# A 31-tap convolution as even and odd outputs that share three half-length filters, with one input buffer

## The chip, the cores and the metric

The kernel runs on one core of a Trainium2 chip. The metric is the device time of one launch in microseconds, as the median of several runs. The core's engines work side by side, each through its own list of instructions, and wait for each other through semaphores: TensorE (PE, matrix products), VectorE (DVE, elementwise work on 128 partitions), ScalarE (ACT, activation functions and copies), GpSimd (POOL, here small square roots and the stores), and SyncE (SP), which issues the loads.

## The reference

One inference step of a two-layer encoder trunk: 2048 prompt frames and 64 sample frames, 1024 channels. Layer 0 is the one that the change touches:

```python
def conv_mixer(h, hist, w_in, conv_w, conv_b, ln_g, ln_b, w_out):
    p = h @ w_in
    a, g_glu, z = jnp.split(p, 3, axis=-1)
    c = a * jax.nn.sigmoid(g_glu)
    c_pad = jnp.concatenate([hist.astype(c.dtype), c], axis=1)
    y = causal_dwconv(c_pad, conv_w, conv_b)          # 31 taps, each channel by itself
    y = jax.nn.silu(layernorm(y, ln_g, ln_b)) * jax.nn.silu(z)
    return y @ w_out, c_pad[:, -CONV_STATE:]
```

Layer 1 is a gated unit with three large products (`u`, `v`, `z`) and a 128x128 mixing of frames. Both layers have a norm before and behind, and a residual sum. All is float32; each large product is made as three products of a high and a low half.

## The kernel before

The frames are cut into two halves: half 0 has 1024 frames (8 tiles of 128), half 1 has 1024 + 64 (9 tiles). Frames lie along the free dimension in the stages A and U, channels on the partitions.

- **Stage A** (to about 600 us) computes the input product of layer 0 in 48 units, n = 0 to 47, 24 for each half. A unit is 128 output channels; three in a row make one block of 128 channels: the sigmoid part (n mod 3 = 0), the linear part (1), whose product with the sigmoid VectorE makes (`cs`, L1074), and `z` (2). A unit has two chunks of 512 frames in half 0 and three of 364, 364 and 360 in half 1. Its weights are loaded (`raw`), rounded by ScalarE to a high half (`Wh`, `a_high`) and subtracted by VectorE for the low half (`Wl`, `a_low(n + 2)`, in unit n). The block is stored to `c_scratch`.
- **The convolution** works on 16 blocks, 8 channel groups for each half. A block is loaded into `cp` (two buffers), 1024 columns wide in half 0 and 1118 in half 1 (prompt, history and sample frames in one). VectorE adds tap by tap into `acc` (two buffers): the first tap is a TENSOR_SCALAR with the bias (L1049), the 30 others are a SCALAR_TENSOR_TENSOR, shifted source times weight plus `acc` (L1053). Each waits for the one before. The block is then stored to `y_scratch` by GpSimd.
- **The plan** (`tap_plan`) spreads the 16x31 taps over VectorE's instruction list: in stage A 3 taps in the units 4 and 5, 7 in the units 6 to 43, 4 in 44 and 45; in stage V 2 or 3 for each tile; in stage U 11 for each `j`. VectorE runs them in that place and in no other.
- **Stage O** follows for half 0: norm, gate and output product of layer 0, tile by tile. Its first pieces are drawn into the last units of stage A: the statistic `o_stats(0, 0)` stands on VectorE right behind the taps of unit 43, and TensorE's second group of transposes of tile 0 stands behind the first chunk of unit 44.
- **Stage V** for half 0 (about 705 to 880 us) computes `v` in four quarters of 8 tiles. VectorE has the low half of the next quarter's weights (`Vl`), the taps and a statistic (`vbs`, L1206) for each tile.
- **Stage U** for half 0 (to about 1280 us) has 16 steps `j`: the products for `u` and `z`, the norm of `v` on VectorE (`vt`, L1224 and L1228), the mixing on TensorE (L1573), the gating (`m`, L1257 and L1272), and taps at three places.
- Then the stages O, V and U of half 1 and the last output product, in which there is no convolution.

SyncE issues the loads in a list of its own. `c_load(b + 2)` stands in the unit where block b ends, behind the weight load of that unit, and waits for block b's last tap. GpSimd's stores of `y` stand likewise in the unit where a block ends.

Of the kernel before, what the change touches and what calls it, by code (L numbers as in the profile page):

```python
# [5 lines left out]
P = 128  # L6
# [20 lines left out]
NCH = (2, 3)  # L27
UNITS_A = 3 * JA
CONV_W = (1024, 1024 + HIST + N_SAMPLE)
NBLK = 2 * JA  # L30
VW = 512
NQ = EB // VW

P_CONVB, P_LNG, P_LNB, P_BG, P_BB = 0, 8, 16, 24, 40
# [4 lines left out]
    return N_SAMPLE if t == NTILES - 1 else P  # L39


def tap_plan():
# [5 lines left out]
    taps, ends, k = {}, {}, 0  # L48
    for key, n in room:
        hi = min(k + n, NBLK * TAPS)  # L50
        taps[key] = (k, hi)
        for b in range(NBLK):
            if k <= TAPS * b + TAPS - 1 < hi:
                ends.setdefault(key, []).append(b)
        k = hi
    assert k == NBLK * TAPS
    return taps, ends


def build(nc, x, wa_in, wa_out, wb_v, wb_uz, wb_out, hist, conv_w, chan_par, pre_g, post_g, b_gb, ws_t, s_bias,  # L60
# [14 lines left out]
    with ctx:  # L75
# [16 lines left out]
        def sem(name):  # L92
            return ctx.enter_context(nc.semaphore(name))
# [5 lines left out]
        par = g("par", [P, NPAR])  # L99
# [30 lines left out]
        r = Region(r1_at, r2_at)  # L130
# [6 lines left out]
        for h in range(2):  # L137
            r = Region(r2_at, c_at)
# [50 lines left out]
        for h in range(2):  # L189
            o = OutBuffers()  # L190
            r = Region(m_at, w_at) if h == 0 else Region(c_at, m_at)
            o.yb = [r(f"yb{h}{i}", [P, KD, P]) for i in range(3)]

            at = r.at
            o.zb, o.sl = [r(f"zb{h}0", [P, KD, P])], [Region(at, top)(f"sl{h}0", [P, KD, P], f32r)]
            o.sh = [r(f"sh{h}0", [P, KD, P], f32r)]
            at = z1_at if h == 0 else m_at
            o.zb.append(Region(at, top)(f"zb{h}1", [P, KD, P]))
            o.sl.append(Region(at, top)(f"sl{h}1", [P, KD, P], f32r))
            r = Region(e_at, top) if h == 0 else Region(m_at + KD * P * 4, w_at)  # L200
            o.xn = [r(f"xo{h}{i}", [P, D]) for i in range(2)]
            r = Region(w_at, e_at)
# [59 lines left out]
        a_cld = [sem(f"a_cld{i}") for i in range(2)]  # L262
        a_yst = [sem(f"a_yst{i}") for i in range(2)]
# [31 lines left out]
        taps_at, conv_ends = tap_plan()  # L295


        def x_slot(t):
# [117 lines left out]
        def _(sp):  # L416
# [10 lines left out]
            def c_load(b):  # L427
                h, j = b // JA, b % JA
                sp.wait_ge(a_cst, c_stored(b))
                if b >= 2:  # L430
                    sp.wait_ge(a_conv, b - 1)
                if h == 0:
                    sp.dma_start(cp[b % 2][:, HIST:HIST + 1024], c_d[j, :, HIST:HIST + 1024]).then_inc(a_cld[b % 2], 16)
                else:
                    sp.wait_ge(ld_hist, 16)
                    sp.dma_start(cp[b % 2][:, :], c_d[j, :, 1024:PADDED]).then_inc(a_cld[b % 2], 16)

            def c_loads(key):
                for b in conv_ends.get(key, []):
                    if b + 2 < NBLK:  # L440
                        c_load(b + 2)

            def wo_load(h, k):
                if k == 0 and h == 0:
# [5 lines left out]
            def o_load_y(t):  # L450
                h = half_of(t)
                if t == TILES[h][0]:
                    for s in range(2):
                        sp.wait_ge(a_yst[s], y_stored(JA * (h + 1) - 2 + s))
# [165 lines left out]
            for n in range(2 * UNITS_A):  # L620
                if n + 3 < 2 * UNITS_A:
                    a_load(n + 3)
                if n == 2:
                    c_load(0)
                for i in (2 * n, 2 * n + 1):
                    if 11 + i < NTILES:
                        x_load(11 + i)
                if n == 5:
                    c_load(1)
# [32 lines left out]
        def _(pool):  # L662
# [26 lines left out]
            def y_stores(key):  # L689
                for b in conv_ends.get(key, []):  # L690
                    h, j = b // JA, b % JA
                    pool.wait_ge(a_conv, b + 1)
                    full, tail = tiled(y_d, h, j)
                    a = acc[b % 2]
                    nc.gpsimd.dma_start(full, a[:, 0:1024].rearrange("p (t n) -> p t n", n=P)).then_inc(a_yst[b % 2], 16)
                    if h == 1:
                        nc.gpsimd.dma_start(tail, a[:, 1024 + HIST:CONV_W[1]]).then_inc(a_yst[b % 2], 16)

            def ln_rsqrt(t):
                pool.wait_ge(o_agg, t + 1)  # L700
# [314 lines left out]
        def _(dve):  # L1015
# [24 lines left out]
            def taps(k0, k1):  # L1040
                for i in range(k0, k1):
                    b, k = i // TAPS, i % TAPS
                    h, j = b // JA, b % JA
                    a, c, w = acc[b % 2][:, 0:CONV_W[h]], cp[b % 2], CONV_W[h]
                    if k == 0:
                        dve.wait_ge(a_cld[b % 2], 16 * (b // 2 + 1))
                        if b >= 2:
                            dve.wait_ge(a_yst[b % 2], y_stored(b - 2))
                        ins = nc.vector.tensor_scalar(a, c[:, 0:w], cw[:, j, 0:1], par[:, P_CONVB + j:P_CONVB + j + 1],  # L1049
                                                      ALU.mult, ALU.add)  # L1050
                    else:
                        dve.wait_ge(a_tap, (TAPS - 1) * b + k)
                        ins = nc.vector.scalar_tensor_tensor(out=a, in0=c[:, k:k + w], scalar=cw[:, j, k:k + 1], in1=a,  # L1053
                                                             op0=ALU.mult, op1=ALU.add)
                    ins.then_inc(a_conv if k == TAPS - 1 else a_tap, 1)

            def fill(key):
                taps(*taps_at.get(key, (0, 0)))

            def a_chunk(n, c):  # L1060
                h, j, m = unit_a(n)
                c0, w = CHUNKS[h][c]
                p = a_pos[n, c]
                k0, k1 = taps_at.get(("A", n), (0, 0))
                taps(k0 + (k1 - k0) * c // NCH[h], k0 + (k1 - k0) * (c + 1) // NCH[h])
                if c == (1 if n < 3 else 0):
                    if 3 <= n + 2 < 2 * UNITS_A:
                        a_low(n + 2)
                    if 26 <= n < 26 + KD:
                        wo_low(0, n - 26)  # L1070
                if m == 1:
                    dve.wait_ge(a_sig, a_count(n - 1, c))
                    dve.wait_ge(a_mm, p + 1)
                    nc.vector.tensor_tensor(cs[:, c0:c0 + w], PS[:, p % A_BANKS, 0:w], cs[:, c0:c0 + w], ALU.mult)\  # L1074
                        .then_inc(a_prod, 1)
                if 0 <= p - 2 < 9:
                    n1_low(6 + p)
                    if 7 + p < NTILES:
                        n1_scale(7 + p)
# [237 lines left out]
            for t in range(8):  # L1317
# [2 lines left out]
                    a_low(t // 2)  # L1320
                if t + 2 < 9:
                    n1_scale(t + 2)
            for i in range(2):
                nc.vector.memset(cp[i][:, 0:HIST], 0.0).then_inc(c_pad, 1)
            dve.wait_ge(ld_par, 16)
            dve.wait_ge(ld_cw, 16)
            dve.wait_ge(c_pad, 2)
# [369 lines left out]
```

## Time and profile before

| | |
|---|---|
| median of 3 runs | 2417.61 us (2415.47 to 2418.39) |
| the profiled execution, its own time | 2414.95 us |
| its span in the profile | 2413.1 us |
| TensorE busy | 2351.5 us, 97% |
| VectorE busy | 1449.3 us, 60% |
| ScalarE busy | 674.6 us, 28% |
| the taps L1053 | 480 operations, 639.4 us |
| granted TensorE clock, mean | 0.99 |

The profile shows for each engine what it did and when, and for each idle stretch what ended it. An arrow as in `PS L1573 <- DVE vt L1228` names who was waited for: here TensorE's work of line 1573 waited for VectorE's result `vt` of line 1228. TensorE is the busiest engine, so a stretch in which it waits is time lost; waits of the others cost nothing by themselves.

### The profile page before, as it was taken

How to read it: one execution, taken by the hardware profiler on the slowest of the kernel's cores; microseconds unless marked ns; L12 is line 12 of the kernel's file. 1: busy time of each engine (PE TensorE's matmuls, PEld its weight loads, DVE VectorE, ACT ScalarE, POOL GpSimd, SP SyncE). 2: the span in 40 equal slices, each digit the busy share in tenths (PEclk: the TensorE clock that was granted, in tenths of full speed). 3: DMA queues.
4: the chain of work that ended last, by engine and by line, in shares of the span. 5: the costliest groups of instructions: out<-in, count | busy, mean ns of one | idle time of the engine just before them, and what ended most of it. 6: DMA issues, size and time to landing. Idle time of an engine off the chain costs nothing.

```text
span 2413.1 us, 27653 instructions
## 1 busy us (share of the span) xinstructions
PE 2351.5 (97%) x11824; PEld 2053.7 (85%) x11824; DVE 1449.3 (60%) x1395; ACT 674.6 (28%) x955; POOL 233.4 (10%) x419
## 2 busy tenths in 40 slices
PE   7899999999999998999989999999999998999998
PEld 6788899999887887888778877889999998888885
DVE  5599999995769879999946742224334444222221
ACT  5322223222542112222324531112222333111110
POOL 1100000001211110000001210011000000000000
PEclk9999999999999999999989999999999999999999
DMA  4323244232552213333334442113222344322220
GB/s 167 122 93 100 98 136 143 94 125 76 185 192 104 95 68 106 112 101 113 126 120 140 137 147 95 65 53 100 85 86 89 116 135 166 110 97 91 92 92 22
DMA packets 113818, 265.05 MB, mean 110 GB/s; under 512 B 15776, under 2 KB 51872, under 8 KB 111648
## 3 DMA queue, kind: packets, MB, share of 16 engines
q1 hardware_dynamic: 90208, 184.64, 23.3%
q0 software_dynamic: 23488, 78.64, 9.5%
q8 instruction: 93, 1.52, 0.3%
q14 instruction: 29, 0.24, 0.0%
HBM read 184.86 MB, written 78.75 MB: 109 GB/s over the span
## 4 chain that ended last, share of the span: by engine, by line
PE 92%; DVE 4%; DMA 2%; ACT 1%; issue 1%; POOL 0%; SPq 0%; DVEq 0%; ACTq 0%
PE PS L1366 29%; PE PS L1367 29%; PE PS L1368 29%; PE PS L1573 3%; DVE acc L1053 2%; PE PS L1412 1%; PE PS L1434 1%; PE PS L1377 1%; DMA raw<-wa_in_in 0%; PE PS L1421 0%; DMA zb<-silu_z_scratch 0%; DMA xt<-x_in 0%; DVE m L1272 0%; DMA rawb<-wb_out_in 0%; DVE Ul L1017 0%
## 5 line engine op out<-in xcount | busy, mean ns | idle before, releaser
L1053 DVE SCALAR_TENSOR_TENSOR acc<-cp,cw,acc 128x1024 f32<-128x1024 f32 (+1 forms) x480 | 639.4, 1332 | 12.6
L1366 PE MATMUL PS<-HBh,Uh 128*128 128x512 f32 (+2 forms) x1280 | 457.6, 357 | 1.6 <-ACT vb L931 1.6
L1367 PE MATMUL PS<-HBl,Uh 128*128 128x512 f32 (+2 forms) x1280 | 453.4, 354 | 0.0
L1368 PE MATMUL PS<-HBh,Ul 128*128 128x512 f32 (+2 forms) x1280 | 453.4, 354 | 0.0
L1366 PE MATMUL PS<-HAh,Wh 128*128 128x512 f32 (+2 forms) x960 | 341.7, 356 | 0.5 <-DVE HAl L1017 0.5
L1367 PE MATMUL PS<-HAl,Wh 128*128 128x512 f32 (+2 forms) x960 | 340.0, 354 | 0.0
L1368 PE MATMUL PS<-HAh,Wl 128*128 128x512 f32 (+2 forms) x960 | 339.8, 354 | 0.0
L1366 PEld LDWEIGHTS PS<-HBh,Uh 128*128 128x128 f32 x1280 | 241.9, 189 | 23.4 <-issue 2.6
L1368 PEld LDWEIGHTS PS<-HBh,Ul 128*128 128x128 f32 x1280 | 241.6, 189 | 20.7
L1367 PEld LDWEIGHTS PS<-HBl,Uh 128*128 128x128 f32 x1280 | 241.8, 189 | 20.0 <-issue 0.2
L1366 PE MATMUL PS<-Wbh,s7h 128*128 128x512 f32 (+1 forms) x544 | 212.6, 391 | 7.4 <-DVE s7l L1017 7.4
L1366 PE MATMUL PS<-Vh,HBh 128*128 128x512 f32 (+1 forms) x544 | 212.5, 391 | 1.8 <-DVE Vl L1017 1.7
L1367 PE MATMUL PS<-Wbl,s7h 128*128 128x512 f32 (+1 forms) x544 | 212.5, 391 | 0.0
L1368 PE MATMUL PS<-Wbh,s7l 128*128 128x512 f32 (+1 forms) x544 | 212.2, 390 | 0.0
L1367 PE MATMUL PS<-Vl,HBh 128*128 128x512 f32 (+1 forms) x544 | 211.8, 389 | 0.0
L1368 PE MATMUL PS<-Vh,HBl 128*128 128x512 f32 (+1 forms) x544 | 211.7, 389 | 0.0
L1366 PEld LDWEIGHTS PS<-HAh,Wh 128*128 128x128 f32 x960 | 181.4, 189 | 15.8 <-issue 0.7
L1368 PEld LDWEIGHTS PS<-HAh,Wl 128*128 128x128 f32 x960 | 181.1, 189 | 15.3
L1367 PEld LDWEIGHTS PS<-HAl,Wh 128*128 128x128 f32 x960 | 181.3, 189 | 14.8
L1353 DVE TENSOR_TENSOR t<-PS,gpb 128x1024 f32<-128x1024 f32 (+1 forms) x17 | 20.8, 1224 | 238.5 <-ACT t7b L797 238.5
L1206 DVE BATCH_NORM_STATS2 vbs<-vb 128x6 f32<-128x512 f32 (+1 forms) x68 | 47.1, 692 | 153.9 <-ACT vb L931 153.7
L947 ACT ACTIVATE sz<-PS 128x512 f32<-128x512 f32 (+2 forms) x80 | 41.8, 523 | 338.6 <-PE PS L1368 338.6
(116 smaller groups left out, 3036.6 us busy)
## 6 DMA issues: line engine op xcount, KB each, us to landing
rawu<-wb_uz_in SPq DMA_DIRECT2D x64, 512.0 KB, 3.5
raw<-wa_in_in SPq DMA_DIRECT2D x48, 512.0 KB, 3.5
rawv<-wb_v_in SPq DMA_DIRECT2D x64, 256.0 KB, 4.8
v_scratch<-vb POOLq DMA_DIRECT2D x64, 256.0 KB, 2.6
vt<-v_scratch SPq DMA_DIRECT2D x32, 512.0 KB, 4.0
s_scratch<-m POOLq DMA_DIRECT2D x32, 512.0 KB, 3.9
st<-s_scratch SPq DMA_DIRECT2D x16, 1024.0 KB, 4.9
xt<-x_in SPq DMA_DIRECT2D x16, 512.0 KB, 4.4
```

Of the source, the lines that this page charges most:

```text
L947: nc.scalar.activation(to[:, c0:c0 + w], PS[:, u_bank(h, p), 0:w], (ACT.Gelu, ACT.Silu)[m])\
L1053: ins = nc.vector.scalar_tensor_tensor(out=a, in0=c[:, k:k + w], scalar=cw[:, j, k:k + 1], in1=a, op0=ALU.mult, op1=ALU.add)
L1206: nc.vector.bn_stats(vbs[0:m, i, q, :], vb[u % 5][0:m, :]).then_inc(v_bn, 1)
L1353: nc.vector.tensor_tensor(t7[0:n, :], banks(2 * b_pair(t))[0:n, :], gpb[0:n, :], ALU.mult).then_inc(b_pm, 1)
L1366: nc.tensor.matmul(out, wh, xh, start=start, stop=False)
L1367: nc.tensor.matmul(out, wh, xl, start=False, stop=False)
L1368: return nc.tensor.matmul(out, wl, xh, start=False, stop=stop)
L1377: last = nc.tensor.transpose(banks(b)[:, k * P:k * P + n], xn[t % 2][0:n, k * P:(k + 1) * P], ident[0:n, 0:n])
L1412: last = nc.tensor.transpose(PS[0:n, 6, k * P:(k + 1) * P], y[:, 4 * half + k, 0:n], ident)
L1434: last = nc.tensor.transpose(banks(4)[:, k * P:k * P + n], ob[half_of(t)].xn[t % 2][0:n, k * P:(k + 1) * P], ident[0:n, 0:n])
L1573: last = nc.tensor.matmul(PS[:, mix_at[h] + i // 4, i % 4 * P:i % 4 * P + n], vt[0:n, i, :], wst[0:n, j // 2, 0:n], start=True, stop=True)
```

## The change

The 31-tap filter is split by the parity of its taps: 16 even ones and 15 odd ones. For each block, with m half the width (512 or 559):

- `pair` is the sum of neighbouring inputs on m + 15 columns (one TENSOR_TENSOR, both sources take every second element).
- The even filter adds 16 taps on m + 1 columns of even inputs into the first half of `acc`; the odd filter adds 15 taps on m columns of odd inputs into the second half. Both read `cp` at every second element, and their first operation is a TENSOR_SCALAR.
- Even outputs: first half + bias + second half, written to every second element of `yc`.
- Odd outputs: `over` = first half moved by one - bias + second half, and then 16 steps with the sums of neighbouring weights (`cg`, made once) on `pair`, the first subtracting `over`; the last writes every second element of `yc`.

That is 50 steps a block on half the columns, where there were 31 on all. All but `pair` wait for the one before them. `cp`, `acc` and the output `yc` are one buffer each: the load of block b + 1 waits until block b has read `cp` for the last time (32 steps done), and block b writes `yc` only when the store of b - 1 has landed. The plan gives 6 steps to the units 4 and 5, 13 to the units 6 to 43, none to 44 and 45; 3 for each tile of stage V's first quarter and 5 in the others; 5, 6 and 6 for each `j` of stage U, until the 800 are done.

```diff
-    room = [(("A", n), 3 if n < 6 else 4 if n >= 44 else 7) for n in range(4, 2 * UNITS_A - 2)]
-    room += [(("V", q, i), 2 if q == 0 or i % 2 == 0 else 3) for q in range(NQ) for i in range(8)]
-    room += [(("U", j, part), n) for j in range(KB) for part, n in enumerate((3, 4, 4))]
+    room = [(("A", n), 6 if n < 6 else 13) for n in range(4, 2 * UNITS_A - 4)]
+    room += [(("V", q, i), 3 if q == 0 else 5) for q in range(NQ) for i in range(8)]
+    room += [(("U", j, part), n) for j in range(KB) for part, n in enumerate((5, 6, 6))]
...
-        cp = [r(f"cp{i}", [P, CONV_W[1] + HIST]) for i in range(2)]
-        acc = [r(f"acc{i}", [P, CONV_W[1]]) for i in range(2)]
+        cp = r("cp", [P, CONV_W[1] + HIST + 2])
+        acc = r("acc", [P, CONV_W[1] + 2])
+        pair = r("pair", [P, CONV_W[1] // 2 + EVEN])
+        over = r("over", [P, CONV_W[1] // 2])
+        yc = r("yc", [P, CONV_W[1]])
...
             def c_load(b):
                 h, j = b // JA, b % JA
                 sp.wait_ge(a_cst, c_stored(b))
-                if b >= 2:
-                    sp.wait_ge(a_conv, b - 1)
+                if b >= 1:
+                    sp.wait_ge(a_tap, (STEPS - 1) * (b - 1) + AT_Y0)
...
+                def taken(at, n):
+                    return cp[:, at:at + 2 * n - 1:2]
+
+                def filtered(out, first, src, w, start):
+                    if start:
+                        return nc.vector.tensor_scalar(out, src, w, None, ALU.mult)
+                    return nc.vector.scalar_tensor_tensor(out=out, in0=src, scalar=w, in1=first, op0=ALU.mult, op1=ALU.add)
+
+                if k == 0:
+                    if b >= 1:
+                        dve.wait_ge(a_conv, b)
+                    dve.wait_ge(a_cld, 16 * (b + 1))
+                    ins = nc.vector.tensor_tensor(pair[:, 0:m + ODD], taken(1, m + ODD), taken(2, m + ODD), ALU.add)
+                else:
+                    dve.wait_ge(a_tap, (STEPS - 1) * b + k)
+                if AT_EVEN <= k < AT_ODD:
+                    i = k - AT_EVEN
+                    ins = filtered(q0, q0, taken(2 * i, m + 1), cw[:, j, 2 * i:2 * i + 1], i == 0)
+                if AT_ODD <= k < AT_Y0:
+                    i = k - AT_ODD
+                    ins = filtered(q1, q1, taken(2 * i + 1, m), cw[:, j, 2 * i + 1:2 * i + 2], i == 0)
+                if k == AT_Y0:
+                    if b >= 1:
+                        dve.wait_ge(a_yst, c_stored(b - 1))
+                    ins = nc.vector.scalar_tensor_tensor(out=yc[:, 0:2 * m:2], in0=acc[:, 0:m], scalar=bias, in1=q1,
+                                                         op0=ALU.add, op1=ALU.add)
+                if k == AT_OVER:
+                    ins = nc.vector.scalar_tensor_tensor(out=over[:, 0:m], in0=acc[:, 1:m + 1], scalar=bias, in1=q1,
+                                                         op0=ALU.subtract, op1=ALU.add)
+                if k >= AT_BOTH:
+                    i = k - AT_BOTH
+                    w = cg[:, j, i:i + 1] if i < ODD else cw[:, j, TAPS - 1:TAPS]
+                    out = over[:, 0:m] if i < ODD else yc[:, 1:2 * m:2]
+                    ins = nc.vector.scalar_tensor_tensor(out=out, in0=pair[:, i:i + m], scalar=w, in1=over[:, 0:m],
+                                                         op0=ALU.mult, op1=ALU.subtract if i == 0 else ALU.add)
+                ins.then_inc(a_conv if k == STEPS - 1 else a_tap, 1)
```

## Rows read from the trace of the kernel before

**Rows 1.** The page: busy time of each engine, its share, instructions.

```profile
PE 2351.5 (97%) x11824; PEld 2053.7 (85%) x11824; DVE 1449.3 (60%) x1395; ACT 674.6 (28%) x955; POOL 233.4 (10%) x419
```

**Rows 2.** TensorE's waits over the span: us in total, times, longest.

```profile
PE PS L1573 <- DVE vt L1228: 8.5, 2, 6.2
...
PE PS L1421 <- DVE rm L1103: 4.9, 1, 4.9
PE PS L1412 <- DVE bst L1095: 4.1, 2, 3.5
PE PS L1366 <- DVE Vl L1017: 1.7, 1, 1.7
```

**Rows 3.** Busy time by stretch, stage A: PE, PEld, DVE, ACT, POOL, clock, DMA.

```profile
121.50:551.30 429.80, 429.80 (x2288) 397.55 (x2287) 401.69 (x344) 109.03 (x132) 31.39 (x45) 1.00 0.33 111
```

**Rows 4.** Groups by form: VectorE's taps and a short operation; busy us, mean ns.

```profile
L1053 DVE SCALAR_TENSOR_TENSOR acc<-cp,cw,acc 128x1118 f32<-128x1118 f32 x240 | 331.4, 1381 | 5.8
L1053 DVE SCALAR_TENSOR_TENSOR acc<-cp,cw,acc 128x1024 f32<-128x1024 f32 x240 | 307.9, 1283 | 6.7
...
L1247 DVE SCALAR_TENSOR_TENSOR addj<-rsb,par,sbb 128x128 f32<-128x128 f32 x32 | 11.0, 344 | 0.0
...
L1049 DVE TENSOR_SCALAR acc<-cp,cw,par 128x1024 f32<-128x1024 f32 x8 | 6.5, 808 | 0.0
```

**Rows 5.** VectorE in order of time, stage A: start, us, operation, [idle before].

```profile
46.75 1.22 DVE L1017 TENSOR_TENSOR HAl<-PS,HAh 128x1024 fp32r<-128x1024 f32 x1 [1.98 <-ACT HAh L810]
...
120.40 1.23 DVE L1017 TENSOR_TENSOR Wl<-raw,Wh 128x1024 fp32r<-128x1024 f32 x1 [3.44 <-ACT Wh L814]
...
219.47 9.20 DVE L1053 SCALAR_TENSOR_TENSOR acc<-cp,cw,acc 128x1024 f32<-128x1024 f32 x7
228.58 1.22 DVE L1017 TENSOR_TENSOR Wl<-raw,Wh 128x1024 fp32r<-128x1024 f32 x1
...
550.60 0.69 DVE L1095 BATCH_NORM_STATS2 bst<-PS 128x6 f32<-128x512 f32 x1
```

**Rows 6.** VectorE's waits from 121.5 to 320 us.

```profile
DVE Wl L1017 <- ACT Wh L814: 8.9, 11, 3.4
```

**Rows 7.** VectorE's waits from 320 to 551.3 us.

```profile
DVE Wl L1017 <- ACT Wh L814: 11.6, 10, 1.9
DVE Wol L1017 <- ACT Woh L842: 3.7, 2, 2.7
```

**Rows 8.** TensorE in order of time, at two places.

```profile
552.93 0.60 PE L1412 MATMUL PS<-con,yb 128*128 128x128 f32 x4
...
923.01 3.78 PE L1573 MATMUL PS<-wst,vt 128*128 128x128 f32 x16 [6.23 <-DVE vt L1228]
```

**Rows 9.** Busy time by stretch behind the longest stop; the clock is third from last.

```profile
919.00:923.00 4.00, 0.00 (x0) 0.00 (x0) 3.93 (x5) 0.00 (x0) 0.00 (x0) 0.50 0.58 219
923.00:929.20 6.20, 6.19 (x23) 5.65 (x24) 6.13 (x7) 0.00 (x0) 1.51 (x2) 0.51 0.15 42
```

**Rows 10.** VectorE in order of time, stage V: first quarter, then a later one.

```profile
728.40 0.67 DVE L1017 TENSOR_TENSOR Vl<-rawv,Vh 128x512 fp32r<-128x512 f32 x1
...
732.31 0.68 DVE L1017 TENSOR_TENSOR Vl<-rawv,Vh 128x512 fp32r<-128x512 f32 x1
...
809.47 0.69 DVE L1206 BATCH_NORM_STATS2 vbs<-vb 128x6 f32<-128x512 f32 x1 [0.87 <-ACT vb L931]
...
814.91 0.69 DVE L1206 BATCH_NORM_STATS2 vbs<-vb 128x6 f32<-128x512 f32 x1
```

**Rows 11.** VectorE in order of time, stage U.

```profile
906.00 1.28 DVE L1257 SCALAR_TENSOR_TENSOR m<-PS,par,addj 128x1024 f32<-128x1024 f32 x1 [5.54 <-PE PS L1573]
...
921.73 1.23 DVE L1228 TENSOR_TENSOR vt<-vt,vrs 128x1024 f32<-128x1024 f32 x1
...
956.28 1.27 DVE L1257 SCALAR_TENSOR_TENSOR m<-PS,par,addj 128x1024 f32<-128x1024 f32 x1
...
980.10 1.28 DVE L1257 SCALAR_TENSOR_TENSOR m<-PS,par,addj 128x1024 f32<-128x1024 f32 x1
...
1222.07 1.23 DVE L1017 TENSOR_TENSOR Ul<-rawu,Uh 128x1024 fp32r<-128x1024 f32 x1 [4.33 <-ACT Uh L904]
```

**Rows 12.** DMA issues: a block's load and store; KB each, us from issue to landing.

```profile
y_scratch<-acc POOLq DMA_DIRECT2D x16, 512.0 KB, 4.5
...
cp<-c_scratch SPq DMA_DIRECT2D x8, 512.0 KB, 4.4
```

More of the change, by code:

```diff
@@ L12 @@
 TAPS = 31
+EVEN, ODD = 16, 15
 HIST = TAPS - 1
@@ L30 @@
 NBLK = 2 * JA
+AT_EVEN, AT_ODD = 1, 1 + EVEN
+AT_Y0 = AT_ODD + ODD
+AT_OVER, AT_BOTH = AT_Y0 + 1, AT_Y0 + 2
+STEPS = AT_BOTH + EVEN
 VW = 512
@@ L39, in rows, with conv_plan @@
     return N_SAMPLE if t == NTILES - 1 else P
-def tap_plan():
-    room = [(("A", n), 3 if n < 6 else 4 if n >= 44 else 7) for n in range(4, 2 * UNITS_A - 2)]
-    room += [(("V", q, i), 2 if q == 0 or i % 2 == 0 else 3) for q in range(NQ) for i in range(8)]
-    room += [(("U", j, part), n) for j in range(KB) for part, n in enumerate((3, 4, 4))]
-    taps, ends, k = {}, {}, 0
+def conv_plan():
+    room = [(("A", n), 6 if n < 6 else 13) for n in range(4, 2 * UNITS_A - 4)]
+    room += [(("V", q, i), 3 if q == 0 else 5) for q in range(NQ) for i in range(8)]
+    room += [(("U", j, part), n) for j in range(KB) for part, n in enumerate((5, 6, 6))]
+    steps, read, ends, k = {}, {}, {}, 0
     for key, n in room:
-        hi = min(k + n, NBLK * TAPS)
-        taps[key] = (k, hi)
+        hi = min(k + n, NBLK * STEPS)
+        steps[key] = (k, hi)
         for b in range(NBLK):
-            if k <= TAPS * b + TAPS - 1 < hi:
+            if k <= STEPS * b + AT_Y0 - 1 < hi:
+                read.setdefault(key, []).append(b)
+            if k <= STEPS * b + STEPS - 1 < hi:
                 ends.setdefault(key, []).append(b)
         k = hi
-    assert k == NBLK * TAPS
-    return taps, ends
+    assert k == NBLK * STEPS
+    return steps, read, ends
 def build(nc, x, wa_in, wa_out, wb_v, wb_uz, wb_out, hist, conv_w, chan_par, pre_g, post_g, b_gb, ws_t, s_bias,
@@ L161, in build @@
         r = Region(c_at, m_at)
[L162 to L163 removed]
+        cp = r("cp", [P, CONV_W[1] + HIST + 2])
[3 more added lines that the diff above has]
+        yc = r("yc", [P, CONV_W[1]])
         cw = r("cw", [P, JA, TAPS])
+        cg = r("cg", [P, JA, ODD])
         r = Region(m_at, top)
@@ L261, in build @@
         a_cst, a_zst, a_tap, a_conv = (sem(f"a_{n}") for n in ("cst", "zst", "tap", "conv"))
-        a_cld = [sem(f"a_cld{i}") for i in range(2)]
-        a_yst = [sem(f"a_yst{i}") for i in range(2)]
+        a_cld, a_yst = sem("a_cld"), sem("a_yst")
         out_conv = sem("out_conv")
@@ L293, in build @@
         b_st = [sem(f"b_st{i}") for i in range(3)]
-        taps_at, conv_ends = tap_plan()
+        steps_at, conv_read, conv_ends = conv_plan()
         def x_slot(t):
@@ L429, in c_load @@
                 sp.wait_ge(a_cst, c_stored(b))
-                if b >= 2:
-                    sp.wait_ge(a_conv, b - 1)
+                if b >= 1:
+                    sp.wait_ge(a_tap, (STEPS - 1) * (b - 1) + AT_Y0)
                 if h == 0:
-                    sp.dma_start(cp[b % 2][:, HIST:HIST + 1024], c_d[j, :, HIST:HIST + 1024]).then_inc(a_cld[b % 2], 16)
+                    sp.dma_start(cp[:, HIST:HIST + 1024], c_d[j, :, HIST:HIST + 1024]).then_inc(a_cld, 16)
                 else:
                     sp.wait_ge(ld_hist, 16)
-                    sp.dma_start(cp[b % 2][:, :], c_d[j, :, 1024:PADDED]).then_inc(a_cld[b % 2], 16)
+                    sp.dma_start(cp[:, 0:CONV_W[1] + HIST], c_d[j, :, 1024:PADDED]).then_inc(a_cld, 16)
             def c_loads(key):
-                for b in conv_ends.get(key, []):
-                    if b + 2 < NBLK:
-                        c_load(b + 2)
+                for b in conv_read.get(key, []):
+                    if b + 1 < NBLK:
+                        c_load(b + 1)
             def wo_load(h, k):
@@ L452, in o_load_y @@
                 if t == TILES[h][0]:
-                    for s in range(2):
-                        sp.wait_ge(a_yst[s], y_stored(JA * (h + 1) - 2 + s))
+                    sp.wait_ge(a_yst, c_stored(JA * (h + 1) - 1))
                     if h == 0:
@@ L693, in y_stores @@
                     full, tail = tiled(y_d, h, j)
-                    a = acc[b % 2]
-                    nc.gpsimd.dma_start(full, a[:, 0:1024].rearrange("p (t n) -> p t n", n=P)).then_inc(a_yst[b % 2], 16)
+                    nc.gpsimd.dma_start(full, yc[:, 0:1024].rearrange("p (t n) -> p t n", n=P)).then_inc(a_yst, 16)
                     if h == 1:
-                        nc.gpsimd.dma_start(tail, a[:, 1024 + HIST:CONV_W[1]]).then_inc(a_yst[b % 2], 16)
+                        nc.gpsimd.dma_start(tail, yc[:, 1024 + HIST:CONV_W[1]]).then_inc(a_yst, 16)
             def ln_rsqrt(t):
@@ L1038, in wo_low, with conv_step @@
                 split_low(Wol[:, k, :], rawo[:, k, :], Woh[:, k, :], wo_lo)
-            def taps(k0, k1):
-                for i in range(k0, k1):
[L1042 to L1055, printed above, removed]
+            def conv_step(b, k):
+                h, j = b // JA, b % JA
+                m = CONV_W[h] // 2
+                q0, q1, bias = acc[:, 0:m + 1], acc[:, m + 1:2 * m + 1], par[:, P_CONVB + j:P_CONVB + j + 1]
+                def taken(at, n):
[32 more added lines that the diff above has]
+                ins.then_inc(a_conv if k == STEPS - 1 else a_tap, 1)
@@ L1057, in fill, with conv_steps @@
+            def conv_steps(k0, k1):
+                for i in range(k0, k1):
+                    conv_step(i // STEPS, i % STEPS)
             def fill(key):
-                taps(*taps_at.get(key, (0, 0)))
+                conv_steps(*steps_at.get(key, (0, 0)))
             def a_chunk(n, c):
@@ L1063, in a_chunk @@
                 p = a_pos[n, c]
-                k0, k1 = taps_at.get(("A", n), (0, 0))
-                taps(k0 + (k1 - k0) * c // NCH[h], k0 + (k1 - k0) * (c + 1) // NCH[h])
+                k0, k1 = steps_at.get(("A", n), (0, 0))
+                conv_steps(k0 + (k1 - k0) * c // NCH[h], k0 + (k1 - k0) * (c + 1) // NCH[h])
                 if c == (1 if n < 3 else 0):
@@ L1322, in _ @@
                     n1_scale(t + 2)
-            for i in range(2):
-                nc.vector.memset(cp[i][:, 0:HIST], 0.0).then_inc(c_pad, 1)
+            for i, n in ((0, HIST), (CONV_W[0] + HIST, 2), (CONV_W[1] + HIST, 2)):
+                nc.vector.memset(cp[:, i:i + n], 0.0).then_inc(c_pad, 1)
             dve.wait_ge(ld_par, 16)
             dve.wait_ge(ld_cw, 16)
-            dve.wait_ge(c_pad, 2)
+            nc.vector.tensor_tensor(cg[:, :, :], cw[:, :, 0:2 * ODD:2], cw[:, :, 1:2 * ODD:2], ALU.add).then_inc(c_pad, 1)
+            dve.wait_ge(c_pad, 4)
             for n, c in a_order:
```

4 lines of the change are left out of this document (removed).

## The prediction

> **What bounds the kernel now.** I read the busy shares first, then what TensorE waited for, then VectorE stage by stage. TensorE is busy for 2351.5 of the 2413.1 us span [rows 1]. So the convolution, which runs on VectorE alone, costs time only where TensorE stands still for it. The list of TensorE's waits [rows 2] has four lines that can touch the convolution: 8.5 us for `vt`, 4.9 us for `rm`, 4.1 us for `bst` and 1.7 us for `Vl`. Everything that the change can win lies in those lines and in the half clock behind them. VectorE busy time as such is worth nothing. What the change can lose is larger: in stage A (to 551 us) TensorE never waits for VectorE after 110 us, but VectorE works 401.7 of 429.8 us there [rows 3], so a fuller share of work in that stage ends in a wait.
>
> **Price of a step.** One tap on 1024 columns takes 1283 ns, one on 1118 takes 1381 ns, and the same operation on 128 columns 344 ns [rows 4]. The slope is (1283-344)/896 = 1.048 ns a column, so a step on 512 columns takes 344+384x1.048 = 746 ns, on 559 columns 796 ns. A step waits for the one before it. Seven taps last 9.20 us [rows 5], so from start to start it is (9.20-1.28)/6 = 1.320 us, 37 ns over the duration. I give the new steps the same 37 ns: 0.783 and 0.833 us. The first operation of a filter has one source; on 1024 columns it takes 808 ns [rows 4]. With half of the 475 ns by which that is cheaper than a tap, it is some 550 ns on 512 columns, 0.59 us with the wait. If a source that takes every second element loses that advantage, it is 0.78 us. The sum `pair` on 527 columns is taken at 0.74 us (a little under a tap of this width).
>
> **A whole block.** Before, narrow: 30x1.320+0.845 = 40.4 us. After: 47x0.783+2x0.59+0.74 = 38.7 us. A wide block goes from 43.4 to 41.1 us. So the change wins 4 to 5% of the convolution, not the quarter that the count of multiplications suggests: 50 steps pay the fixed 0.25 us where 31 did. That alone moves nothing on TensorE.
>
> **What it moves: the plan.** Units 6 to 43 of stage A took 7 taps each, 266 in all. They now take 13 steps each, 494 in all. Work goes from stage U into stage A.
> Before: 235 narrow taps x1.320 = 310.2, 7 narrow firsts 5.9, 23 wide taps x1.417 = 32.6, one wide first 0.9: 349.6 us.
> After (steps 12 to 505: 388 in narrow blocks, 106 in wide ones): 366x0.783 + 15x0.59 + 7x0.74 = 300.7, and 98x0.833 + 5x0.61 + 3x0.79 = 87.0: 387.7 us.
> That is 38.1 us more for VectorE in these units.
> VectorE's free time there is what it waits for ScalarE's high halves: 8.9 us [rows 6], of which 3.4 us lie ahead of unit 6 [rows 5], and 11.6+3.7 us [rows 7]. That makes 20.8 us. An operation that does not wait starts 0.09 us before the end of the one in front (219.47 to 228.58 is 9.11 us where the taps last 9.20, [rows 5]), so each of the 21 waits gives 0.09 us more when it closes: 22.7 us. The other 38.1-22.7 = 15.4 us make VectorE late at the end of unit 43.
>
> **Who waits for that.** Inside the stage nobody: `Wl` of unit n+2 is ready over a unit (10.9 us) before TensorE needs it, about 13.6 us in the narrow half and 17 in the wide one, as ScalarE rounds it early in unit n. The banks leave more. The first one to feel it is the `bst` statistic of tile 0, which stands on VectorE right behind unit 43's steps. It ended at 551.3 us [rows 5], and TensorE reached the transposes that need it at 552.93 us [rows 8], 1.6 us later. So TensorE stands still for 15.4-1.6 = 13.8 us. Units 44 and 45, which had four taps each, have no steps now, so VectorE is free behind that and it is not paid twice. After a stop the clock is low: in 923 to 929.2 us the granted clock was 0.51 [rows 9] behind a stop of 6.2 us, which cost about 3.1 us. I add 3 us. **Stage A: +16.8 us.**
>
> **Stage V.** With two taps a tile, the stretch from one `Vl` to the next was 3.91 us [rows 10]. Three steps instead take 0.34 us less (3x0.833 against 2x1.417), over seven tiles 2.4 us, and the wait of 1.7 us for `Vl` [rows 2] is gone. In the later quarters a tile with three taps takes 5.44 us from statistic to statistic [rows 10], which is TensorE's own pace. Five steps are 4.16 us against 4.25, so 5.35 us: they fit, with 0.09 us to spare on 24 tiles. **V: -1.7 us.**
>
> **Stage U.** From 906.00 to the end of `vt` at 922.96 us VectorE did seven taps and the rest, and TensorE waited 6.2 us for it [rows 8, 11]. Now eleven steps stand there: 11x0.833 = 9.2 us against 9.9, so 0.7 us less; the clock drop behind it stays. The period of a `j` was 23.82 us [rows 11] with eleven taps (15.6 us); with 17 steps it is 14.2, so 22.4 us, under TensorE's 23.7. The steps end in j = 8 instead of the taps in j = 12, so the 2.2 us of the second `vt` wait [rows 2] go. The waits for `rm` and `bst` near 1220 and 1250 us stay: there `Ul` had itself waited 4.33 us for ScalarE [rows 11], not for a tap. **U: -2.9 us.**
>
> **Small things at nothing.** `cg` and one more fill are under 0.5 us on VectorE at about 44 us. Behind them it idled 1.98 us for ScalarE before `HAl` [rows 5], which covers them; without that cover they would cost their 0.5 us once. With one input buffer, the load of the next block starts after step 32. The 18 steps that follow last 14 us, the load 4.4 us [rows 12], and it goes out late only where SP stands behind a raw weight load. SP may stand up to one unit behind VectorE's step, with weight loads queued behind it; they are needed two units later. The single `yc` has 32 steps (25 us) for its store of 4.5 us. If that cover fails, every block pays up to 4 us and the 16 blocks up to 60; I take zero, since the first need is 10 us away. POOL's stores keep their places.
>
> **Sum.** +16.8-1.7-2.9 = +12.2 us. Against the profiled execution's 2414.95 us this is 2427; the median of the three runs is 2.7 us above that execution, so I say 2430 us, 0.5% slower.
>
> **The stride.** The filters read every second element, and two steps write so. No row here has such a pattern on VectorE. The bounds are nothing, and one column more for each strided column (1.05 ns); I stand at nothing, since every form in the trace, shifted, spread or from PSUM, lies on the same slope. The Trainium skill speaks on both sides. SBUF — State Buffer (Door 1: The DMA port swizzle) says that two accesses in one 16-byte line keep full bandwidth, so a step of two floats is free. Vector Engine (DVE) Microarchitecture Reference (5.2 Measured stream behaviour on trn2) says that a port wants runs of two adjacent words from an 8-byte boundary and that hopping each element costs about 0.65 cycle, by which an estimate for this kernel is some 2600 us. No run yet shows which holds.
>
> **Rivals.**
> *The stride costs.* Two thirds of the steps have a strided operand. At a third of a column (0.35 ns) a step is 0.12 us longer on average: stage A +60 us, V five steps a tile 0.6 us longer against 0.09 spare, +13 us, U 24.5 against 23.7 us a `j`, +7 us; in all about 2510 us, and with a whole column some 2700. Against it speaks only the even slope. Chance 0.2. It would show as step durations over 0.85 us.
> *A step is cheaper than the line says, and the stop does not form.* If the fixed part of a short dependent step (0.25 us) is lower by 0.028 us, that is 0.755 instead of 0.783 us, 494 steps give back the 13.8 us; there is no stop, no half clock, and V and U leave -4.6 us: 2413 us, just not slower or a little faster. For it: the 37 ns and the fixed part come from long operations, and only one row is short. Against it: 344 ns for 128 columns is on the line. Chance 0.17. From 0.755 us it decides the sign.
> *The change does not bring its work saving*, as stalls on the single buffers eat it: 2440 to 2480 us. Chance 0.05; the 14 and 25 us of room speak against it.
>
> **How the numbers follow.** My forecast has 0.58: lag 11 to 20 us at unit 43, which is 2424 to 2440 us; its top end has the one-source operations at 0.78 us (+3.8 us) and a stop that is counted without the 2.2 us of overlap. The range of 2411 to 2450 takes in the cheap step and the lower part of the buffer case and leaves the costly stride out. Faster and slower mean by over 0.2% (4.8 us), which is about what a measurement of this kernel can tell from no change. A cheap step gives half its chance to faster and half to the same, with some of my forecast's low end in the same: 0.10, 0.15, 0.75.
>
> **What would show it.** Steps at 746 and 796 ns with 37 ns between them; VectorE's waits for `Wh` gone between unit 10 and unit 43; a new TensorE wait for `bst` near 553 us of 10 to 16 us, with a half clock around it; no wait for `Vl` near 747 us; the `vt` wait near 935 us still 5 to 6 us; no second `vt` wait; `rm` and `bst` waits unchanged. It is wrong if the durations differ by over 25 ns, if TensorE waits for `Wl` or if VectorE waits for `cp`.

## The result, and the profile after

The changed kernel takes 2422.85 us (median of 11 runs, 2420.41 to 2427.35), the kernel before 2414.82 us (11 runs): a ratio of 1.0029, interval 1.0020 to 1.0038. Measured once more beside an experiment below, it was 1.0036 (1.0023 to 1.0049). So it is slower by 7 to 9 us, where 12 were forecast. The direction and the new stop came as forecast. The size did not, and a part of it comes from short waits in stage U that the forecast left out.

The page of the changed kernel; the first line answers to [rows 1]:

```profile
span 2421.2 us, 27975 instructions
...
PE 2350.7 (97%) x11824; PEld 2055.8 (85%) x11824; DVE 1409.9 (58%) x1701; ACT 672.9 (28%) x955; POOL 235.1 (10%) x419
```

VectorE works 39 us less and TensorE as long as before, yet the span of the profile is 8.1 us longer. What TensorE waited for answers to [rows 2]:

```profile
PE PS L1448 <- DVE bst L1129: 18.4, 3, 14.5
PE PS L1402 <- DVE s7l L1022: 6.5, 2, 4.8
PE PS L1457 <- DVE rm L1137: 5.6, 2, 4.9
PE PS L1609 <- DVE vt L1262: 5.2, 1, 5.2
```

The wait for `Vl` and the second one for `vt` are gone, the first one for `vt` fell from 6.2 to 5.2 us, and there is a new stop of 14.5 us for `bst`. The groups by form answer to [rows 4] (busy us, mean ns, idle before):

```profile
L1056 DVE SCALAR_TENSOR_TENSOR acc<-cp,cw,acc 128x513 f32<-128x513 f32 x120 | 90.4, 754 | 3.7
L1083 DVE SCALAR_TENSOR_TENSOR over<-pair,cg,over 128x512 f32<-128x512 f32 x120 | 90.1, 751 | 3.8
...
L1083 DVE SCALAR_TENSOR_TENSOR over<-pair,cg,over 128x559 f32<-128x559 f32 x120 | 96.0, 800 | 3.5
...
L1056 DVE SCALAR_TENSOR_TENSOR acc<-cp,cw,acc 128x512 f32<-128x512 f32 x112 | 84.3, 753 | 3.6
L1083 DVE SCALAR_TENSOR_TENSOR yc<-pair,cw,over 128x559 f32<-128x559 f32 x8 | 6.4, 804 | 0.3
...
L1055 DVE TENSOR_SCALAR acc<-cp,cw 128x560 f32<-128x560 f32 x8 | 4.7, 582 | 0.2
...
L1055 DVE TENSOR_SCALAR acc<-cp,cw 128x512 f32<-128x512 f32 x8 | 3.9, 487 | 0.2
```

A step that reads every second element of `cp` takes 753 ns on 512 columns, one that reads `pair` without gaps takes 751, and a write to every second element of `yc` 804 against 800 on 559 columns. So the stride costs nothing here. The Trainium skill's page SBUF — State Buffer (Door 1: The DMA port swizzle), by which two floats in one 16-byte line keep the rate, agrees. The 0.65 cycle that the Trainium skill's page Vector Engine (DVE) Microarchitecture Reference (5.2 Measured stream behaviour on trn2) puts on hopping with every element does not hold for a step of two; no run here shows larger hops.

VectorE in order of time at the end of unit 43, and TensorE at the same place, answer to [rows 5] and [rows 8]:

```profile
549.13 10.84 DVE L1083 SCALAR_TENSOR_TENSOR over<-pair,cg,over 128x559 f32<-128x559 f32 x13
559.88 1.22 DVE L1022 TENSOR_TENSOR Wl<-raw,Wh 128x1024 fp32r<-128x1024 f32 x1
...
569.30 0.69 DVE L1129 BATCH_NORM_STATS2 bst<-PS 128x6 f32<-128x512 f32 x1
```

```profile
570.04 1.11 PE L1448 MATMUL PS<-con,yb 128*128 128x128 f32 x4 [14.53 <-DVE bst L1129]
```

Thirteen steps take 10.84 us, from start to start (10.84-0.80)/12 = 0.837 us. TensorE was at its transposes at 555.5 us and stood until 570.0. In stage A, VectorE now waits only once, in the window from 121.5 to 320 us (us, times, longest), and not at all from 320 to 575 us, where [rows 6, 7] had 20.8 us behind unit 6:

```profile
DVE Wl L1022 <- ACT Wh L819: 3.2, 1, 3.2
```

The stretches behind the stop, with the granted clock third from last, answer to [rows 9]:

```profile
570.00:576.10 6.10, 6.06 (x22) 6.06 (x23) 2.02 (x3) 0.00 (x0) 2.18 (x4) 0.52 0.58 183
576.10:582.00 5.90, 5.90 (x39) 5.87 (x38) 0.00 (x0) 1.06 (x3) 0.00 (x0) 1.00 0.00 0
```

Six microseconds at the lower level of 1.2 GHz cost 3 us, as much as behind the shorter stop of the kernel before. Last, stage U (answers to [rows 11]), from the mixing of j = 0 to the norm of `v` for j = 1, with eleven steps on two places (six are shown):

```profile
923.91 1.28 DVE L1291 SCALAR_TENSOR_TENSOR m<-PS,par,addj 128x1024 f32<-128x1024 f32 x1 [6.20 <-PE PS L1609]
...
927.58 4.98 DVE L1056 SCALAR_TENSOR_TENSOR acc<-cp,cw,acc 128x560 f32<-128x560 f32 x6
...
938.63 1.23 DVE L1262 TENSOR_TENSOR vt<-vt,vrs 128x1024 f32<-128x1024 f32 x1
```

**Where the time went.** TensorE's instructions are the same in all these kernels, so the same instruction can be looked up in two traces. The table has its time from TensorE's first instruction, less that in the kernel before (us; worked out from the traces). The columns are single executions: the kernel before again, the changed kernel three times, and the one with 12 steps (below).

| TensorE's place, time before | before again | after | after, 2nd | after, 3rd | 12 steps, 2nd |
|---|---|---|---|---|---|
| 108 us, stage A runs | 0.4 | 2.4 | 2.0 | 1.9 | 0.1 |
| 553 us, ahead of the transposes | 0.4 | 2.4 | 2.0 | 1.8 | 0.1 |
| 553 us, at them | 0.4 | 17.1 | 16.8 | 16.6 | 0.1 |
| 576 us | 0.5 | 19.9 | 19.7 | 19.2 | 0.1 |
| 749 us, second quarter of V | 0.3 | 18.1 | 17.7 | 18.2 | 0.3 |
| 923 us, mixing of j = 1 | 0.3 | 16.9 | 16.6 | 17.1 | 0.5 |
| 949 us | 0.2 | 16.3 | 16.0 | 16.0 | 0.4 |
| 1116 us | 0.2 | 15.0 | 14.7 | 14.7 | -0.8 |
| 1189 us, mixing of j = 12 | 0.2 | 12.5 | 12.2 | 12.2 | -3.4 |
| 1299 us | 0.1 | 9.3 | 12.0 | 11.2 | -3.2 |
| end | -1.0 | 8.1 | 10.7 | 9.9 | -4.4 |

### The profile page after: what moved, and what is told of

Read it like the earlier page. It is cut to its first block, busy times and chain, and to the rows that moved or that the text cites. A ratio compares the mean times of both kernels' runs of the same rounds, so it can differ in the third digit from the quotient of the medians.

```text
span 2421.2 us, 27975 instructions
## 1 busy us (share of the span) xinstructions
PE 2350.7 (97%) x11824; PEld 2055.8 (85%) x11824; DVE 1409.9 (58%) x1701; ACT 672.9 (28%) x955; POOL 235.1 (10%) x419
## 4 chain that ended last, share of the span: by engine, by line
PE 78%; DVE 17%; issue 2%; DMA 2%; ACT 1%; POOL 0%; SPq 0%; DVEq 0%; ACTq 0%
PE PS L1402 25%; PE PS L1403 24%; PE PS L1404 24%; DVE acc L1056 7%; DVE over L1083 4%; PE PS L1609 3%; DVE Wl L1022 2%; DVE cs L1108 1%; PE PS L1448 1%; PE PS L1470 1%; PE PS L1413 1%; DMA raw<-wa_in_in 0%; DVE Wol L1022 0%; DVE acc L1055 0%; PE PS L1457 0%
## 5 line engine op out<-in xcount | busy, mean ns | idle before, releaser
L1056 DVE SCALAR_TENSOR_TENSOR acc<-cp,cw,acc 128x513 f32<-128x513 f32 (+3 forms) x464 | 360.4, 777 | 14.0
L1404 PEld LDWEIGHTS PS<-HAh,Wl 128*128 128x128 f32 x960 | 182.2, 190 | 15.4
L1083 DVE SCALAR_TENSOR_TENSOR over<-pair,cg,over 128x512 f32<-128x512 f32 (+1 forms) x240 | 186.1, 775 | 7.3
L1389 DVE TENSOR_TENSOR t<-PS,gpb 128x1024 f32<-128x1024 f32 (+1 forms) x17 | 20.8, 1224 | 237.1 <-ACT t7b L802 237.1
L1291 DVE SCALAR_TENSOR_TENSOR m<-PS,par,addj 128x1024 f32<-128x1024 f32 x32 | 41.0, 1283 | 163.4 <-PE PS L1609 163.4
```

Of the source, the lines that this page charges most:

```text
L1056: return nc.vector.scalar_tensor_tensor(out=out, in0=src, scalar=w, in1=first, op0=ALU.mult, op1=ALU.add)
L1083: ins = nc.vector.scalar_tensor_tensor(out=out, in0=pair[:, i:i + m], scalar=w, in1=over[:, 0:m], op0=ALU.mult, op1=ALU.subtract if i == 0 ...
L1291: ins = nc.vector.scalar_tensor_tensor(out=m6[:, 0:1024].rearrange("p (a n) -> p a n", n=P), in0=banks(b).rearrange("p (a n) -> p a n", n= ...
L1404: return nc.tensor.matmul(out, wl, xh, start=False, stop=stop)
```

## The experiments

**Is it the lateness at unit 43? One step less for each unit.**

```diff
-    room = [(("A", n), 6 if n < 6 else 13) for n in range(4, 2 * UNITS_A - 4)]
+    room = [(("A", n), 6 if n < 6 else 12) for n in range(4, 2 * UNITS_A - 4)]
```

> The changed kernel with 12 steps instead of 13 in the units 6 to 43 of stage A; the 38 steps go to stage U, which ends three j later. Theory (the loss is VectorE's lateness at unit 43): 38 x 0.79 = 30 us less work in stage A is more than the 16 us of lateness, so TensorE's wait of 14.5 us for bst near 555 us is gone and with it the half clock behind it (2.7 us); what is left are the gains in stages V and U, 5 to 8 us, so the ratio to the kernel before is 0.997 to 0.998. Rival (the single buffers or the form of the steps cost the time): the wait shrinks by no more than the 0.8 us of the step taken out of unit 43, and the ratio stays at 1.002 or above.

Measured: 2410.17 us, ratio 0.9981 (0.9973 to 0.9990). TensorE's waits:

```profile
PE PS L1609 <- DVE vt L1262: 5.5, 1, 5.5
PE PS L1457 <- DVE rm L1137: 4.9, 1, 4.9
PE PS L1448 <- DVE bst L1129: 4.1, 2, 3.5
...
PE PS L1402 <- DVE Vl L1022: 1.3, 1, 1.3
```

The long stop is gone; the 3.5 us for `bst` that are left are those that the kernel before has near 1224 us. With one number of the plan changed the same convolution is faster than the old one, by 0.2%. The rival falls: buffers and steps are those of the changed kernel. To size the difference by times, both ran again on one chip.

> The changed kernel once more, beside the one with 12 steps on the same chip, to size the step from 13 to 12 by times instead of by one trace. The traces give 14 us between the two by the middle of stage U (wait 14.3, half clock 2.7, rm 0.7 us, less what the kernel with 12 steps waits more in stages O and V, about 3 us); the ratios measured so far, 1.0029 and 0.9981, give 11.6 us with 3 us of error. If the traces hold: 1.0030 to 1.0040 here.

> The kernel with 12 steps again: 0.9975 to 0.9985, so 13 to 14 us under the changed kernel; if the time between the two is under 11 us, a part of the wait at unit 43 is given back somewhere that the traces do not name.

Measured: 1.0036 (1.0023 to 1.0049) and 0.9983 (0.9974 to 0.9993), 12.8 us apart. The table gives 14.3 us at the end, two of them from the start-up. So the 17 us of stop and half clock are not all lost. A TensorE that comes late to the stages O and V finds its tiles loaded and its weights ready. The kernel with 12 steps waits in stage V for `Vl` (1.3 us in its first profile, 0.7 in its second), and in stage O for a load of `yb` (1.0 and 2.2 us); the changed kernel waits for neither.

**Does only the new form bring the stop? More of the old taps.**

```diff
-    room = [(("A", n), 3 if n < 6 else 4 if n >= 44 else 7) for n in range(4, 2 * UNITS_A - 2)]
+    room = [(("A", n), 3 if n < 6 else 4 if n >= 44 else 8 if n >= 24 else 7) for n in range(4, 2 * UNITS_A - 2)]
```

> The kernel before with 8 taps instead of 7 in the units 24 to 43; filter and buffers unchanged. Theory: 20 taps more are 26.5 us; VectorE's waits there were 15.3 us, 1.9 us more with the overlap, so it is 9 us late at unit 43 and TensorE waits 7 to 8 us for bst, plus some 3 us of half clock; the taps end earlier in stage U, which takes the second vt wait (2.2 us) away: +6 to +9 us, ratio 1.003. Rival (only the new form of the convolution brings the wait): no bst wait above 1 us, ratio 0.999 to 1.000.

Measured: 2429.8 us, ratio 1.0061 (1.0048 to 1.0074). The place is right, but the stop is twice as long as expected. TensorE's wait, and then VectorE's waits from 320 to 570 us:

```profile
PE PS L1412 <- DVE bst L1095: 20.4, 3, 16.3
```

```profile
DVE Wol L1017 <- ACT Woh L842: 6.8, 2, 4.8
```

Two things were left out of the sum. The twenty taps more all fall on wide blocks, 19 at 1.417 us and a first one at 0.9, which makes 27.8 us and not 26.5. And of the 15.3 us of free time in these units only 8.5 could be used, with 0.9 us of overlap where ten of the twelve waits closed: VectorE still waited 6.8 us, now for `Woh`. SyncE's list around the longer of the two waits shows why:

```profile
346.27 0.33 SPq L425 DMA_DIRECT2D raw<-wa_in_in  x1
348.93 0.33 SPq L433 DMA_DIRECT2D cp<-c_scratch  x1
349.30 1.06 SPq L448 DMA_DIRECT2D rawo<-wa_out_in  x1
```

The load of `cp` stood until VectorE's last tap of a block, and the weight load behind it in the list stood with it. With 27.8 us more and 8.5+0.9 us used, lateness is 18.4 us and the stop, 1.6 us less, 16.8; 16.3 were measured. The late engine made its own supply late. That SyncE's order is the cause is read from the trace; it was not tried by itself.

**Place or amount? The steps of unit 43 in unit 46.**

```diff
-    room = [(("A", n), 6 if n < 6 else 13) for n in range(4, 2 * UNITS_A - 4)]
+    room = [(("A", n), 6 if n < 6 else 13) for n in (*range(4, 43), 46)]
```

> The changed kernel with the 13 steps of unit 43 moved to unit 46; stage A as a whole has as many steps as in the changed kernel. Theory (the lateness at the one place behind unit 43 is what costs): 13 steps are 10.7 us, so the wait for bst falls from 14.5 to about 4 us, and in unit 46 the steps lie in an idle stretch of 12 us: 10 to 11 us faster than the changed kernel, ratio to the kernel before 0.998 to 1.000. Rival (the amount of convolution work in stage A decides, wherever it stands): the ratio stays at 1.002 or above.

Measured: 2418.25 us, ratio 1.0016 (1.0006 to 1.0026). TensorE's waits between 553 and 640 us:

```profile
PE PS L1448 <- DVE bst L1129: 4.3, 1, 4.3
PE PS L1457 <- DVE rm L1137: 4.2, 1, 4.2
```

The stop shrank from 14.5 to 4.3 us as expected, with as many steps in stage A as in the changed kernel, so it is the place that counts. The time alone does not show it: 0.998 to 1.000 was expected, and the interval reaches over the rival's 1.002. The reason is a second stop of 4.2 us, which I had not seen. The idle stretch of unit 46 was idle on VectorE only. Its last product `cs` came later, GpSimd stores it, waits for the landing, and only then makes the root that `rm` needs:

```profile
606.32 0.64 POOL L683 DMA_DIRECT2D c_scratch<-cs  x1 [22.99 <-DVE cs L1108]
...
613.31 0.88 POOL L776 DMA_DIRECT2D conv_out_dram<-c_scratch  x1 [2.93 <-DMA c_scratch<-cs]
...
615.44 0.57 POOL L672 TENSOR_TENSOR rs<-mv,half_neg 128x1 f32<-128x1 f32 x1
```

**What does the convolution cost at all?**

```diff
-                        ins = nc.vector.scalar_tensor_tensor(out=a, in0=c[:, k:k + w], scalar=cw[:, j, k:k + 1], in1=a,
+                        ins = nc.vector.scalar_tensor_tensor(out=a[:, 0:64], in0=c[:, k:k + 64], scalar=cw[:, j, k:k + 1], in1=a[:, 0:64],
```

> The kernel before with every tap but the first on 64 columns only, all instructions and waits in place: this leaves most of the convolution out and shows what the convolution costs at all. Theory (it costs only where TensorE waits): the vt waits (8.5 us), the Vl wait (1.7 us) and the half clock behind the long vt wait (3 us) go, the rm and bst waits at 1220 and 1250 us stay: 13 us less, ratio 0.9945. Rival (VectorE's traffic also slows TensorE or the waits for rm and bst come from the taps too): 20 us less or more.

Measured: 2401.32 us, ratio 0.9944 (0.9929 to 0.9958), 13.5 us less. Its waits for `rm` and `bst` are those of the kernel before:

```profile
PE PS L1421 <- DVE rm L1103: 4.9, 1, 4.9
PE PS L1412 <- DVE bst L1095: 4.1, 2, 3.5
```

The kernel leaves most columns of the filter out: of 653 us of VectorE's work on it, 149 us are left, and TensorE waits for none of them. So the convolution cost 13.5 us of time, and in these places no cheaper form of it could win more.

**The places in stage U.** These two start from the kernel with 12 steps. First the steps that stand between the mixing of j = 0 and the norm for j = 1 go elsewhere, then also the order of VectorE's list changes where stage O of half 1 begins:

```diff
-    room += [(("U", j, part), n) for j in range(KB) for part, n in enumerate((5, 6, 6))]
+    room += [(("U", j, part), 0 if (j, part) in ((0, 2), (1, 0)) else n) for j in range(KB) for part, n in enumerate((5, 6, 6))]
```

> The changed kernel with 12 steps in the units 6 to 43 and no steps at the two places of stage U between the mixing of j = 0 and the norm of v for j = 1 (where 11 stood). Theory: the norm of v of j = 1 is ready 9.2 us earlier, before TensorE needs it; its wait of 5.5 us for vt goes, and the half clock behind it (2.5 to 3 us): ratio 0.9981 - 0.0034 = 0.9947. Rival (another work on VectorE comes late in its place, or the clock falls anyway): ratio 0.997 or above.

Measured: 2400.09 us, ratio 0.9946 (0.9933 to 0.9959), where 0.9947 was expected. `vt` is no longer in TensorE's list.

```diff
-                    if 2 * j + 3 < 2 * KB:
-                        u_low(n + 3)
                     if h == 0 and j >= KB - 3:
                         o_step(1, j - KB)
+                    if 2 * j + 3 < 2 * KB:
+                        u_low(n + 3)
```

> As the kernel with 12 steps and the gap, and in the last three j of stage U the first pieces of stage O of half 1 stand ahead of the low half of the next weights (Ul) on VectorE instead of behind it. Theory: the waits for bst (3.5 us) and rm (4.9 us) near 1220 and 1250 us come from Ul, which waits for ScalarE, and not from the convolution; both go, with 2.5 us of half clock behind each: 13 us less than with the gap alone, ratio 0.989. Rival (they wait for the transposes and GpSimd's root anyway): ratio 0.993 or above.

Measured: 2386.46 us, ratio 0.9892 (0.9877 to 0.9907). TensorE's largest waits outside the start-up are now these:

```profile
PE PS L1402 <- DVE s7l L1022: 6.3, 2, 4.8
PE PS L1402 <- ACT vb L936: 1.6, 2, 0.8
```

**The same places with the old convolution.** The kernel before with that gap (its taps moved to stage V, three for each tile of the last three quarters) and that order:

> The kernel before, filter and buffers unchanged (31 taps on all columns), with the same gap in stage U (the taps between the mixing of j = 0 and the norm of v for j = 1 are moved to stage V, where every tile of the last three quarters now has three), and the same order of stage O's first pieces ahead of Ul. Theory (the form of the convolution is worth next to nothing to TensorE, the places are worth all): the first vt wait with its half clock (9 us) and the waits for rm and bst with theirs (13 us) go; the second vt wait of 2.2 us may stay, since this plan has VectorE full until j = 12: ratio 0.990 to 0.991, within 0.002 of the changed kernel with the same places. Rival (the cheaper convolution is what made those places free): ratio 0.994 or above.

> The changed kernel with 12 steps, gap and order once more, beside the kernel above on the same chip: ratio 0.989 again within 0.0015, and 2 to 4 us under it.

Measured on one chip: 2394.0 us, ratio 0.9912 (0.9898 to 0.9927), and 2389.17 us, 0.9892 (0.9875 to 0.9908). Two waits remain in the old form that the new one lacks:

```profile
PE PS L1573 <- DVE vt L1228: 2.3, 1, 2.3
PE PS L1412 <- DVE bst L1095: 2.1, 1, 2.1
```

The places are worth 21 us with the old filter. The new one adds 5 us where both are planned alike (2 to 4 were expected), though the two intervals overlap.

**Profiles taken again.** The two kernels, unchanged:

> The kernel before, unchanged, for a second profile. Theory: TensorE's waits repeat within 1 us; where the clock stands low repeats only in part, so the time at which stage A begins to run steadily and the half clock near 1225 and 1255 us differ from the first profile by up to 3 us each. Rival (the differences of the first two profiles outside the waits are due to the change): they repeat within 0.5 us.

> The changed kernel, unchanged, for a second profile. Theory: TensorE's wait for bst near 555 us is 14 to 15 us again and vt's 5.2 us; the stretches at half clock behind 1225 us, which the first profile had shorter than the kernel before by 2.3 us, come back in part, since they are luck of the single execution. Rival (they are an effect of the change): they are as short as in the first profile within 0.5 us.

TensorE's waits came back within 0.3 us, but for those of the start-up and of the last stage, which moved by about a microsecond. The stretches at half clock did not. Between 1189 and 1299 us the first profile of the changed kernel gained 3.2 us on the kernel before, the second one 0.2 us (table). The same stretch around the end of the `bst` wait, 1234.3 to 1241.1 us, in the first and in the second profile:

```profile
1234.30:1241.10 6.80, 4.78 (x23) 4.05 (x24) 4.09 (x4) 1.04 (x2) 0.00 (x0) 1.00 0.01 2
```

```profile
1234.30:1241.10 6.80, 5.57 (x16) 4.56 (x17) 3.43 (x4) 0.25 (x1) 0.00 (x0) 0.52 0.01 2
```

## Why the prediction was wrong in its size

- **TensorE bounds the kernel and the convolution costs only where it waits.** Right: 13.5 us in all, by the kernel with short taps.
- **Price of a step.** Right: 753 and 800 ns were measured for 746 and 796, and 0.787 (thirteen in 10.19 us) and 0.837 us from start to start for 0.783 and 0.833. The first operations took 487 to 582 ns in the mean for 550; the 550 was a slip, since half of 475 ns off 746 is 509 (0.8 us over the 20 of them in stage A). The convolution's busy time fell by 40 us.
- **Stage A, lateness 15.4 us, stop 13.8 us, half clock 3 us.** Right: 14.5 and 3 us; in the table 14.7 for the stop and 2.8 behind it. The free time was used up to the last. A wait of 0.7 us for `rm` soon after went past the sum, and the lateness covers the 0.5 us for `yb` that the kernel before has. What the stop gives back against the kernel with 12 steps, some 3 us, is no part of this difference beyond that. (The rows have 22 waits that close, not 21, and the overlap is 1.9 to 2.0 us; the 2.2 us named under the chances is a slip.)
- **Stage V, -1.7 us.** Right: 1.8 to 2.0 us at the `Vl` near 749 us, and the kernel with 12 steps, which has no stop, gains the same there. The 0.09 us to spare in the later quarters was too little without the stop: that kernel waits for `Vl` again at 837 us, the 1.3 and 0.7 us named above.
- **Stage U, -2.9 us: this term failed.** The table has -1.2 us at the mixing of j = 1, -0.6 behind it, -1.3 by 1116 us and -2.5 at j = 12: 5.5 us. The two waits themselves were nearly right (1.0 for 0.7, 2.2 for 2.2). Left out were a shorter half clock behind the first, and 1.3 us that TensorE's mixings lose while VectorE is full and `vt` comes just in time. The kernel with short taps has that 1.3 us too (-10.3 at 949 us, -11.6 at 1116), so it belongs to VectorE's load. The weight loads of the mixings (PEld) wait for `vt`, each too briefly for the list of TensorE's waits; in the kernel before, from 945 to 1180 us:

```profile
PEld PS L1573 <- DVE vt L1228: 2.4, 8, 0.4
```

  At these eight mixings TensorE begins 0.05 to 0.10 us after `vt` is done and takes 1.76 or 1.81 us from the first matrix product to what follows, where a `vt` ready 0.57 us earlier gives 1.70 us. The changed kernel has no such wait. The step that failed: the prediction itself put VectorE's period of a `j` at 23.82 us and TensorE's at 23.7, and booked nothing for VectorE being the slower one.
- **The sum.** Without the start-up A, V and U make +10.1 to +10.3 us for the +12.2 forecast, and the times say 7 to 9. The +12.2 to +12.5 that the traces read at 1189 us look like the forecast, but that is luck: 2 us of them arose at the start-up, for which the sum has no term. The full clock set in at 27.2 to 29.8 us in the three profiles of the changed kernel, at 24.5 and 24.8 in those of the kernel before, and at 22.9 to 27.7 in the others. Six profiles of kernels that are the changed one up to unit 5 stand at -0.5 to 0.3 us at 108 us, against its 1.9 to 2.4. So no instruction of the change makes the 2 us; why they came three times out of three stays open. If every run has them, the part without a name is 2 us larger. What is left, 1 to 3 us, is of the size by which single executions differ through the half clock, and I can't place it.
- **The base.** 2430 was built on a median of three runs, 2417.61; with eleven it is 2414.82. So 2.8 us of the distance between 2430 and the measured 2422.85 us come from the base; the forecast difference of 12.2 us stands against a measured one of 8.0.
- **The rivals.** The stride costs nothing. A step is not cheaper than the line. The single buffers never made VectorE wait for `cp`.

## What to carry to other kernels

When work that fills an engine's gaps is planned, count it against the free time of each stage and look at the first item behind it in that engine's list that another engine needs: 38 us more over 38 units, of which some 22 found free time, cost nothing until one statistic, and then 14.5 us at once. An idle stretch of one engine is free only if nothing behind it in the list is on a path through other queues. A cheaper form of hidden work is worth little by itself; moving eleven of its steps and one group of instructions off the two places where TensorE waited won five times as much.

## What was not expected of the hardware

- Behind a stop of 14.5 us the clock was low for 6 us of TensorE's work, no longer than behind one of 6.2 us; in single executions of the same kernel such a stretch came or did not (0.52 against 1.00 above), at a cost of up to 2.5 us each.
- The one-source operation that begins the even filter takes 582 ns in the mean on 560 columns, the one of the odd filter 508 ns on 559; both read every second element. The difference lies in single operations: of the 32 in the profile 27 take 482 to 514 ns, and the five longer ones (619 to 875 ns) are just those in which GpSimd's issue of a store of `yc` (L700) comes to its end. Here one of each kind:

```profile
517.32 0.90 POOL L700 DMA_DIRECT2D y_scratch<-yc  x1 [17.79 <-DVE yc L1083]
...
517.86 0.62 DVE L1055 TENSOR_SCALAR acc<-cp,cw 128x560 f32<-128x560 f32 x1
...
565.09 0.50 DVE L1055 TENSOR_SCALAR acc<-cp,cw 128x560 f32<-128x560 f32 x1
```

  In both other profiles of this kernel it is the same five. The two-source steps that read `cp` never take over 806 ns. That the store makes them longer is read from this coincidence; it was not tried by itself.
